# Prompt attention on one core: bias and minimum in one VectorE operation, fp32r scores, units ordered by pairs of heads

## The chip, the cores and the metric

The kernel runs on one core of a Trainium2 chip. The metric is the device time of one execution in microseconds; the profile is one further execution, recorded by the hardware profiler. PE is TensorE, DVE VectorE, ACT ScalarE, POOL GpSimd, SP the engine that issues most transfers.

## What is computed

The program is one step of a one-layer decoder with 1024 prompt tokens and 8 short samples. The change lies in the prompt's sparse attention (8 query heads, 2 groups of key heads, width 64) and in the projection that feeds it. For each head and token there are three softmaxes: over compressed blocks of keys (cmp), over all earlier keys (sel: the 16 blocks of 64 are all chosen at this length), and over a window of 512 (win):

```python
def masked_softmax(s, mask):
    s = jnp.where(mask, s.astype(jnp.float32), -1e30)
    m = jnp.max(s, axis=-1, keepdims=True)
    e = jnp.where(mask, jnp.exp(s - m), 0.0)
    return e / jnp.maximum(jnp.sum(e, axis=-1, keepdims=True), 1e-30)

def attend_shared(q, q_pos, k, v, k_pos, mask, rel_bias):
    s = jnp.einsum('...qgrd,...kgd->...qgrk', q, k).astype(jnp.float32) * (HEAD_DIM ** -0.5)
    dist = q_pos[..., :, None] - k_pos[..., None, :]
    bias = rel_bias[rel_bucket(dist)]
...
    p = masked_softmax(s + bias, mask[..., :, None, None, :])
    o = jnp.einsum('...qgrk,...kgd->...qgrd', p.astype(v.dtype), v)
    return o, p
```

The three outputs are weighted by gates and added.

## The kernel before

`program` runs seven stages in turn: projection, prompt attention, the state-space mixer (SSD), sample attention, output projection, and two feed-forward stages. Each stage is a block in which every engine has its own list of instructions, joined by semaphores that are written by hand; a block ends when all its engines have.

*Projection* (`stage_project`, L181). 17 column blocks of `w_in`, each in three pieces of 352 tokens, are multiplied on PE as fp32r parts (L470). Blocks of kind NORM give keys and queries; for each of their pieces ACT takes the square root (L680) and DVE a reciprocal (L937) and a scaling (L944, L955). Finished keys lie in `ev` by feature; SP copies them four times per branch, to both halves of the partitions of `m.kd` (`double_keys`, L370). At the end SP loads the bias table `m.bias` (L433) and the first queries (L177).

*Prompt attention* (`stage_prompt_attention`, L1437). A unit is one tile t of 128 tokens, one key group g and one pair of heads rp; there are 32, with tiles in the order 1, 3, 5, 7, 6, 4, 2, 0 and the four units of a tile one after the other. A unit has four steps i: sel for either head, then win with cmp for either head. Step n = 4u + i uses PSUM banks 0 and 1 or 2 and 3 by turns.

- `scores` (PE, L1566, L1569): the keys of a row are cut in half; either half is a matmul with 64 rows of the array, rows 0 to 63 or 64 to 127, in plain fp32. It waits until ACT's exponentials of step n - 2 have left the banks.
- `add_bias` and `prepare` (DVE): the bias is added in PSUM to the last 256 keys at most (L1704; farther keys all fall in the last bucket, which is subtracted from the table), the far mask to the first 128 of a full window, and the negated maximum is taken (L1714, L1717, L1719).
- `exps` (ACT, L1645, L1649): exponential from PSUM to the ring `psel` or `pwc` of three units, with the sum accumulated.
- `rate` (DVE, L1727, L1728) inverts the sums, and POOL multiplies the rows by that and the gate (L1671, L1676).
- Two units behind, `turn` (PE, L1582) transposes the rows in fills of two key tiles for both heads, `copy` (ACT, L1627) takes a fill from banks 4 to 6 to `pt` (4 slots), and `weigh` (PE, L1596) multiplies it with the values, adding into bank 7, from which `take_o` (DVE, L1734) takes a finished unit to `m.mix`. A unit of tile t has (t + 1) + min(t, 4) + 1 key tiles and one compressed one; tile 7 has 7 fills, all units together 160.

The order on PE is written out in one loop, with `LAG = 2` fills between a transpose and its weighting:

```python
for f in share(u - BEHIND, i):
    turn(u - BEHIND, f)
    behind.append((u - BEHIND, f))
    if len(behind) > LAG:
        weigh(*behind.popleft())
```

SP meanwhile loads queries for later tiles, gates by row (16 transfers), the samples' compression weights and states.

## Time and profile before

| | us |
|---|---|
| median of 3 runs | 1928.62 (1927.55 to 1933.23) |
| the profiled execution | 1937.85 |
| its span, first to last instruction | 1936.1 |
| PE busy in the span | 1781.6 (92%) |
| DVE busy | 1051.9 (54%) |
| ACT busy | 732.5 (38%) |
| POOL busy | 361.7 (19%) |

Times are microseconds, ns where marked. Busy PE counts a matmul from its start to a modelled end, and successive ones overlap, so start times tell more than durations. PE's matmuls are listed as PE, its weight loads as PEld. In lists by line, the columns are line, engine, operation, what is written and read, shapes, count, busy us, mean ns of one, and the idle time of the engine just before with what ended it.

### The profile page before, as it was taken

The numbers are of one execution on the slowest core, as the hardware profiler recorded it, in microseconds if no ns is written. First come the engines' busy times: TensorE is split into PE (matmuls) and PEld (weight loads), VectorE is DVE, ScalarE is ACT, GpSimd is POOL, SyncE is SP. The second block draws the span as 40 slices with busy tenths as digits, with TensorE's granted clock in tenths as the row PEclk, the third lists the DMA queues.
The fourth block names the chain that finished last, engine by engine and source line by source line (L and its number), as shares of the span: only waits on it lengthen the run. The fifth ranks groups of instructions, "written<-read, shape, count | busy, mean of one in ns | idle before, by whom it ended". The sixth has DMA issues, their size and how long they took to land. (4 is left out here: it accounts for less than half of the span.)

```text
span 1936.1 us, 33115 instructions
## 1 busy us (share of the span) xinstructions
PE 1781.6 (92%) x12217; PEld 1459.9 (75%) x12217; DVE 1051.9 (54%) x2339; ACT 732.5 (38%) x1546; POOL 361.7 (19%) x424
## 2 busy tenths in 40 slices
PE   6999997999999958998986997899999999899998
PEld 5999996666666645654654785899999999788885
DVE  6632167766666664556453457767677766541221
ACT  5413533676774233355332333333322332331111
POOL 1422111444344435325241000000000000100000
PEclk9999997899997988999988998899999999999999
DMA  5533141300000018637484322121222211832320
GB/s 149 98 119 86 36 99 29 66 12 12 13 14 1 6 43 321 199 131 267 154 276 155 122 80 90 53 79 66 87 77 69 96 66 45 324 92 60 98 90 24
DMA packets 160411, 188.92 MB, mean 98 GB/s; under 512 B 49727, under 2 KB 126184, under 8 KB 160235
## 3 DMA queue, kind: packets, MB, share of 16 engines
q1 hardware_dynamic: 139842, 114.00, 20.3%
q0 software_dynamic: 19872, 72.36, 10.8%
q8 instruction: 71, 1.16, 0.2%
q10 hardware_dynamic: 584, 1.06, 0.1%
q14 instruction: 42, 0.34, 0.1%
HBM read 156.30 MB, written 28.99 MB: 96 GB/s over the span
## 5 line engine op out<-in xcount | busy, mean ns | idle before, releaser
L2788 PE MATMUL banks<-u_sum,w_sum 128*128 128x264 f32 x3696 | 456.7, 286 | 16.3 <-DVE u_sum L2831 10.3
L2788 PEld LDWEIGHTS banks<-u_sum,w_sum 128*128 128x128 f32 x3696 | 455.5, 191 | 17.3 <-issue 9.1
L470 PE MATMUL banks<-u_parts_mix,w_in_parts 128*128 128x352 f32 x1440 | 244.3, 327 | 4.4 <-DVE u_parts_mix L826 4.4
L470 PEld LDWEIGHTS banks<-u_parts_mix,w_in_parts 128*128 128x128 f32 x1440 | 231.3, 189 | 7.8 <-DVE u_parts_mix L826 4.8
L3052 PE MATMUL banks<-w_down_hi,g_parts 128*128 128x512 f32 x704 | 218.9, 392 | 8.0 <-DVE g_parts L3087 8.0
L3052 PEld LDWEIGHTS banks<-w_down_hi,g_parts 128*128 128x128 f32 x704 | 133.1, 189 | 36.3 <-DVE w_down_lo L3083 7.7
L2088 ACT ACTIVATE turned<-banks 128x512 f32<-128x512 f32 (+1 forms) x136 | 78.7, 588 | 174.1 <-PE banks L1953 111.9
L1965 PE MATMUL banks<-turned,cmp_w 128*128 128x512 f32 x256 | 133.0, 601 | 7.2 <-DVE turned L2090 4.6
L3052 PE MATMUL banks<-w_down_lo,g_parts 128*128 128x512 f32 x352 | 137.7, 391 | 0.0
L3087 DVE TENSOR_TENSOR g_parts<-g_rows,g_parts 128x256 fp32r<-128x256 f32 (+1 forms) x99 | 39.1, 402 | 177.2 <-ACT g_parts L3020 177.0
L1953 PEld LDWEIGHTS banks<-consts,rows_grouped 128*128 128x128 f32 x512 | 64.7, 144 | 89.7 <-issue 58.8
L2961 POOL DMA_DIRECT2D w_down_whole<-in_w_down x10 | 5.3, 560 | 623.7 <-POOLq L129 623.7
L1627 ACT ACTIVATE p_T<-banks 128x512 f32<-128x512 f32 (+7 forms) x168 | 90.4, 543 | 64.3 <-PE banks L1582 63.4
L3020 ACT ACTIVATE g_parts<-g_rows 128x256 fp32r<-128x256 f32 (+1 forms) x99 | 38.6, 398 | 200.2 <-PE banks L3052 170.8
L1566 PE MATMUL banks<-keys_twice,q_twice 64*128 64x320 f32 (+7 forms) x512 | 99.5, 470 | 14.6 <-ACT p_win_cmp L1649 6.6
L1704 DVE TENSOR_TENSOR banks<-banks,bias 128x256 f32<-128x256 f32 (+6 forms) x240 | 64.2, 298 | 89.4 <-PE banks L1569 49.4
L2515 PE MATMUL banks<-w_out,mixT 128*128 128x512 f32 (+1 forms) x432 | 104.3, 399 | 5.8 <-DVE w_out L2536 5.8
L1953 PE MATMUL banks<-consts,rows_grouped 128*128 128x128 f32 x512 | 78.8, 279 | 30.5 <-DVE rows_grouped L2183 26.9
L2515 PEld LDWEIGHTS banks<-w_out,mixT 128*128 128x128 f32 (+1 forms) x432 | 77.4, 182 | 29.4 <-DVE w_out L2536 5.6
L1596 PE MATMUL banks<-p_T,v 128*64 128x128 f32 x1056 | 91.4, 294 | 2.6 <-DVE mix L1734 1.9
L1714 DVE TENSOR_REDUCE neg_max<-banks 128x1 f32<-128x640 f32 (+7 forms) x128 | 90.6, 708 | 4.4
L2725 ACT ACTIVATE w_sum<-w_whole 128x512 fp32r<-128x512 f32 x110 | 66.3, 623 | 69.5 <-DVE w_whole L2807 69.5
(404 smaller groups left out, 2817.9 us busy)
## 6 DMA issues: line engine op xcount, KB each, us to landing
w_gate_raw<-in_w_gate SPq DMA_DIRECT2D x11, 1024.0 KB, 5.6
w_up_raw<-in_w_up SPq DMA_DIRECT2D x11, 1024.0 KB
g_rows<-g_by_feature SPq DMA_DIRECT2D x88, 128.0 KB, 2.9
g_by_feature<-silu_gate SPq DMA_DIRECT2D x21, 528.0 KB, 3.2
w_in_raw<-in_w_in SPq DMA_DIRECT2D x29, 256.0 KB, 3.4
w_down_whole<-in_w_down SPq DMA_DIRECT2D x12, 512.0 KB, 11.5
w_down_whole<-in_w_down POOLq DMA_DIRECT2D x10, 512.0 KB, 16.4
x_tile<-in_x_prompt SPq DMA_DIRECT2D x8, 512.0 KB, 4.4
```

Source lines behind the costliest of these rows:

```text
L470: mm = nc.tensor.matmul(bank[:, 0:PIECE], w[:, pb, :], u[:, pa, k, tokens(p)], start=(k == 0 and (pa, pb) == TERMS[0]), stop=(k == KT - 1 ...
L1566: mm = nc.tensor.matmul(m.bank[2 * (n % 2) + h][:, 0:b - a], q[rows, :], m.kd[rows, branch, g, lo + a:lo + b], start=True, stop=True)
L1596: mm = nc.tensor.matmul(m.bank[7][64 * r:64 * r + 64, 0:P], x, pt[0:width, F % SLOTS_P, k, r, :], start=(br == SEL and kt == 0), stop=(br ...
L1627: x = nc.scalar.activation(to, have, ACT.Copy) if by_act[F] else nc.vector.tensor_copy(to, have)
L1714: x = nc.vector.tensor_reduce(negmax[:, u, r, br:br + 1], region(i, n, keys), AX.XY, ALU.max, negate=True)
L1953: x = nc.tensor.transpose(m.bank[3 + f % 3][0:width, k * P:(k + 1) * P], src, c("ident"))
L1965: mm = nc.tensor.matmul(m.bank[u % 2][:, :], m.cmp.w1[:, u % 2, q, :, :].rearrange("p j h -> p (j h)"), w.fill[:, f % SLOTS, :], start=(q ...
L2088: x = nc.scalar.activation(to, src, ACT.Copy)
L2515: mm = nc.tensor.matmul(m.bank[2 * (j % 2) + h][0:r, :], mT[:, j % 2, a, k, 0:r], wo[:, b, k, h * 512:(h + 1) * 512], start=(k == 0 and (a ...
L2725: nc.scalar.activation(wp[side, p][:, HI, :, :], src, ACT.Copy).then_inc(s.w_hi, 1)
L2788: mm = nc.tensor.matmul(bank(tg, i), wp[side, p][:, a, k, :], m.u[tg, i, b][:, k, :], start=(k == 0 and (a, b) == TERMS[0]), stop=(k == kh ...
L3052: mm = nc.tensor.matmul(m.bank[i.banks[h]][0:i.rows, :], gp[:, q % RG, pa, k, 0:i.rows], (whi, wlo)[pb][:, f, cols], start=(f == 0 and (pa ...
```

## The change

- **Scores** are fp32r. Queries are split by POOL into a high part and the rest (`split_queries`), keys into high parts on partitions 0 to 63 and low parts on 64 to 127 of `m.kd`, by ACT (`keys_hi`) and DVE (`keys_lo`) in the projection stage; the queries lie on both halves. A score is then two matmuls with all 128 rows, over up to 512 keys each. Keys are negated. SP's eight copies of keys are gone.
- **Bias and minimum.** The table holds the negated bias for the full width of 1024 keys (zero but for the last 256) of one pair of heads, in two slots. One fused DVE operation adds it to the negated scores, writes the sum to `psel` or `pwc` and keeps the minimum, which a second instruction writes out. ACT exponentiates there in place with scale -1. PE waits for `prepared` of step n - 2 instead of `exp_done`.
- **Units** go through all eight tiles for one pair of heads, then the next pair. The table of pair k is loaded by SP during pair k - 1 (8 transfers).
- **Weighted sums** are issued in bursts, when 6 fills have been transposed, of all but 2; `pt` has 8 slots, four of them in `m.mix`. Bank 7 has four places for outputs. Every fourth copy is DVE's.
- The samples' compression weights are loaded at the start of the SSD stage; `ssdn` moves into `m.mix`.

```diff
-Q_SLOTS = 4
+Q_RAW, Q_UNITS = 2, 4
 BCOPIES = 16
 T_ORDER = (1, 3, 5, 7, 6, 4, 2, 0)
-Q_PAIRS = [(t, g) for t in T_ORDER for g in range(NG)]
+HEAD_PAIRS = [(g, rp) for rp in range(2) for g in range(NG)]
+UNITS = [(t, g, rp) for g, rp in HEAD_PAIRS for t in T_ORDER]
...
+def load_table(sp, m, k, sem):
+    g, rp = HEAD_PAIRS[k]
+    for p0 in range(0, P, BCOPIES):
+        at = (g * REP + 2 * rp) * BCOPIES * BIASW + 127 - p0
+        sp.dma_start(m.table[p0:p0 + BCOPIES, k % 2, :, SEQ - 256:SEQ],
+                     bass.AP(m.negbias_dram.tensor, at, [[BIASW - 1, BCOPIES], [BCOPIES * BIASW, 2], [1, 256]])).then_inc(sem, 16)
...
+                def keys_hi(b):
+                    br, src = blocks[b][1] // 2 - 1, ev[:, slot_of[b], 3:3 + SEQ]
+                    act.wait_ge(s.keys_done, br + 1)
+                    if br == 0:
+                        act.wait_ge(s.cmp_summed, 2)
+                    nc.scalar.activation(m.kd[0:64, br, 0, :], src[0:64, :], ACT.Copy, scale=-1.0)
+                    nc.scalar.activation(m.kd[64:P, br, 1, :], src[64:P, :], ACT.Copy, scale=-1.0).then_inc(s.keys_hi, 1)
+                    nc.scalar.activation(m.kd[0:64, br, 1, :], src[64:P, :], ACT.Copy, scale=-1.0).then_inc(s.keys_split, 1)
...
+                def keys_lo(b):
+                    br, src = blocks[b][1] // 2 - 1, ev[:, slot_of[b], 3:3 + SEQ]
+                    dve.wait_ge(s.keys_hi, br + 1)
+                    nc.vector.scalar_tensor_tensor(m.kd[64:P, br, 0, :], src[0:64, :], -1.0, m.kd[0:64, br, 0, :].bitcast(F32),
+                                                   ALU.mult, ALU.subtract)
+                    nc.vector.scalar_tensor_tensor(m.kd[64:P, br, 1, :], src[64:P, :], -1.0, m.kd[64:P, br, 1, :].bitcast(F32),
+                                                   ALU.mult, ALU.subtract).then_inc(s.keys_split, 1)
...
-                sp.wait_ge(m.keys_in, 16 * 8)
-                sp.wait_ge(s.bias_stored, 16)
-                for p0 in range(0, P, BCOPIES):
-                    sp.dma_start(m.bias[p0:p0 + BCOPIES, :, :],
-                                 bass.AP(m.bias_dram.tensor, 127 - p0, [[BIASW - 1, BCOPIES], [BCOPIES * BIASW, NH], [1, 256]])
-                                 ).then_inc(s.bias_loaded, 16)
+                sp.wait_ge(s.bias_stored, 32)
+                sp.wait_ge(s.keys_split, 2 * 2)
                 sp.wait_ge(s.taken_v, taken_before[last_item[SECOND_Q]])
-                for q in range(2):
-                    double_queries(sp, m, q, 0).then_inc(m.q_first, 16)
-                    double_queries(sp, m, q, 0, 1).then_inc(m.q_first, 16)
+                for u0 in range(Q_RAW):
+                    for half in range(2):
+                        double_queries(sp, m, u0, half).then_inc(m.q_first, 16)
+                parted(sp, 2 * len(blocks) - 1)
+                for k in range(2):
+                    load_table(sp, m, k, s.bias_loaded)
...
-    LAG = 2
-    by_act = [True for F in range(first_fill[-1])]
+    LAG, TOGETHER_P, O_SLOTS = 2, 4, 4
+    by_act = [F % 4 != 3 for F in range(first_fill[-1])]
...
+    weighed_at, turned_at, pending = {}, {}, deque()
+    for u in range(U + BEHIND):
+        for i in range(4):
+            for f in share(u - BEHIND, i) if u >= BEHIND else ():
+                pending.append((u - BEHIND, f))
+            weighed_at[u, i] = []
+            if len(pending) >= LAG + TOGETHER_P or (u, i) == (U + BEHIND - 1, 3):
+                while len(pending) > (LAG if (u, i) != (U + BEHIND - 1, 3) else 0):
+                    weighed_at[u, i].append(pending.popleft())
...
                     t, g, rp = units[u]
-                    n, branch, r = 4 * u + i, i // 2, 2 * rp + i % 2
-                    q = qd[:, (u // 2) % QS, r, :]
...
+                    n, branch = 4 * u + i, i // 2
+                    pe.wait_ge(s.q_split, u + 1)
                     if n >= 2:
-                        pe.wait_ge(s.exp_done, n - 1)
-                    keys = (t + 1) * P if branch == 0 else win_tiles(t) * P
+                        pe.wait_ge(s.prepared, n - 1)
+                    keys = keys_of(t, branch)
                     lo = (t + 1) * P - keys
-                    for h, (a, b) in enumerate(halves(keys)):
-                        rows = slice(64 * h, 64 * h + 64)
-                        mm = nc.tensor.matmul(m.bank[2 * (n % 2) + h][:, 0:b - a], q[rows, :],
-                                              m.kd[rows, branch, g, lo + a:lo + b], start=True, stop=True)
+                    parts = [(m.bank[2 * (n % 2) + h][:, 0:b - a], m.kd[:, branch, g, lo + a:lo + b])
+                             for h, (a, b) in enumerate(halves(keys))]
                     if branch == 1:
-                        mm = nc.tensor.matmul(m.bank[2 * (n % 2)][:, 384:384 + cmp_keys(t)], q[0:64, :],
-                                              m.kcd[0:64, g, 0:cmp_keys(t)], start=True, stop=True)
+                        at = cmp_at(n)
+                        parts.append((m.psum[:, at:at + cmp_keys(t) + 1], m.kcd[:, g, 0:cmp_keys(t) + 1]))
+                    for out, k in parts:
+                        for part in (HI, LO):
+                            mm = nc.tensor.matmul(out, qs[:, u % Q_UNITS, part, i % 2, :], k, start=part == HI, stop=part == LO)
                     mm.then_inc(s.scored, 1)
...
-                behind = deque()
+                ended = 0
                 for u in range(U + BEHIND):
                     for i in range(4):
                         if u < U:
...
                         if u >= BEHIND:
                             for f in share(u - BEHIND, i):
                                 turn(u - BEHIND, f)
-                                behind.append((u - BEHIND, f))
-                                if len(behind) > LAG:
-                                    weigh(*behind.popleft())
-                while behind:
-                    weigh(*behind.popleft())
+                        if weighed_at[u, i] and ended:
+                            pe.wait_ge(s.o_taken, ended)
+                        for v, f in weighed_at[u, i]:
+                            weigh(v, f)
+                        ended += len(ends_at[u, i])
...
-                    if u >= RING_P:
-                        act.wait_ge(s.turned, first_fill[u - RING_P + 1])
-                    keys = (t + 1) * P if branch == 0 else win_tiles(t) * P
-                    br, dst = (SEL, psel) if branch == 0 else (WINB, pwc)
-                    x = nc.scalar.activation(dst[:, u % RING_P, r, 0:keys].rearrange("p (h k) -> p h k", h=2), region(i, n, keys),
-                                             ACT.Exp, bias=negmax[:, u, r, br:br + 1], accum_out=sums[:, u, r, br:br + 1])
+                    br, ring = (SEL, psel) if branch == 0 else (WINB, pwc)
+                    p = ring[:, u % RING_P, r, 0:keys_of(t, branch)]
+                    x = nc.scalar.activation(p, p, ACT.Exp, scale=-1.0, bias=negmax[:, u, r, br:br + 1],
+                                             accum_out=sums[:, u, r, br:br + 1])
...
+                def split_queries(u):
+                    if u >= Q_RAW:
+                        pool.wait_ge(s.q_loaded[u % Q_RAW], 32 * (u // Q_RAW))
+                    else:
+                        pool.wait_ge(m.q_first, 16 * 4)
+                    if u >= Q_UNITS:
+                        pool.wait_ge(s.scored, 4 * (u - Q_UNITS + 1))
+                    raw, part = qd[:, u % Q_RAW, :, :], qs[:, u % Q_UNITS, :, :, :]
+                    chain(nc.gpsimd.tensor_copy(part[:, HI, :, :], raw))
+                    nc.gpsimd.tensor_tensor(part[:, LO, :, :], raw, part[:, HI, :, :].bitcast(F32),
+                                            ALU.subtract).then_inc(s.q_split, 1)
+                split_queries(0)
+                nc.gpsimd.memset(m.table[:, :, :, 0:SEQ - 256], 0.0).then_inc(s.zeroed, 1)
+                for u in range(1, 3):
+                    split_queries(u)
...
-                def add_bias(u, i):
...
                 def prepare(u, i):
                     t, g, rp = units[u]
                     n, branch, r = 4 * u + i, i // 2, i % 2
+                    k = HEAD_PAIRS.index((g, rp))
+                    table = m.table[:, k % 2, r, :]
+                    keys = keys_of(t, branch)
+                    br, ring = (SEL, psel) if branch == 0 else (WINB, pwc)
+                    start, at = 1024 * (n % 2), cmp_at(n)
+                    if i == 0:
+                        if u >= RING_P:
+                            dve.wait_ge(s.turned, first_fill[u - RING_P + 1])
+                        if u == 1:
+                            dve.wait_ge(s.zeroed, 1)
+                        if k >= 2 and u % 8 == 0:
+                            dve.wait_ge(s.table_in[k - 2], 16 * (P // BCOPIES))
                     dve.wait_ge(s.scored, n + 1)
-                    add_bias(u, i)
-                    keys = (t + 1) * P if branch == 0 else win_tiles(t) * P
-                    br = SEL if branch == 0 else WINB
-                    x = nc.vector.tensor_reduce(negmax[:, u, r, br:br + 1], region(i, n, keys), AX.XY, ALU.max, negate=True)
                     if branch == 1:
-                        at = 1024 * (n % 2) + 384
-                        chain(nc.vector.tensor_reduce(negmax[:, u, r, CMP:CMP + 1], m.psum[:, at:at + cmp_keys(t)], AX.X,
-                                                      ALU.max, negate=True))
-                        x = nc.vector.tensor_scalar(negmax[:, u, r, CMP:CMP + 1], negmax[:, u, r, CMP:CMP + 1], 1e29, None,
-                                                    ALU.min)
-                    x.then_inc(s.prepared, 1)
+                        if t >= 4:
+                            old = m.psum[:, start:start + P]
+                            nc.vector.tensor_tensor(old, old, c("far"), ALU.subtract)
+                        chain(nc.vector.tensor_tensor_reduce(
+                            pwc[:, u % RING_P, r, CC:CC + cmp_keys(t)], m.psum[:, at:at + cmp_keys(t)],
+                            table[:, 927 - P * t:SEQ:16], 1.0, 3e38, ALU.add, ALU.min,
+                            negmax[:, u, r, CMP:CMP + 1]))
+                        nc.vector.tensor_scalar(negmax[:, u, r, CMP:CMP + 1], negmax[:, u, r, CMP:CMP + 1], 1e29, None,
+                                                ALU.min)
+                    mx = nc.vector.tensor_tensor_reduce(ring[:, u % RING_P, r, 0:keys], m.psum[:, start:start + keys],
+                                                        table[:, SEQ - keys:SEQ], 1.0, 3e38, ALU.add, ALU.min,
+                                                        negmax[:, u, r, br:br + 1])
+                    mx.then_inc(s.prepared, 1)
```

The order of PE in a unit of tile 7. Before (`keys_twice,q_twice` are scores, `consts,p_sel` transposes of the sel rows, `p_T,v` weighted sums):

```order
L1566 MATMUL banks<-keys_twice,q_twice 128x512 x2
L1582 MATMUL banks<-consts,p_sel 128x128 x4
L1596 MATMUL banks<-p_T,v 64x128 x4
L1566 MATMUL banks<-keys_twice,q_twice 128x512 x2
L1582 MATMUL banks<-consts,p_sel 128x128 x4
L1596 MATMUL banks<-p_T,v 64x128 x2
L1596 MATMUL banks<-p_T,vc 64x128 x2
L1582 MATMUL banks<-consts,p_sel 128x128 x4
L1596 MATMUL banks<-p_T,v 64x128 x4
L1566 MATMUL banks<-keys_twice,q_twice 128x320 x2
```

And with the change, in the second half of tile 7's unit and the start of tile 6's, whose fills are those of tiles 3 and 5 (`kc_parts` are the compressed keys):

```order
L1616 MATMUL banks<-consts,p_sel 128x128 x4
L1604 MATMUL banks<-key_parts,q_parts 128x512 x2
L1604 MATMUL banks<-key_parts,q_parts 128x128 x2
L1604 MATMUL banks<-kc_parts,q_parts 128x64 x2
L1616 MATMUL banks<-consts,p_win_cmp 128x128 x4
L1629 MATMUL banks<-p_T,v 64x128 x8
L1629 MATMUL banks<-p_T,vc 64x128 x2
L1629 MATMUL banks<-p_T,v 64x128 x4
L1604 MATMUL banks<-key_parts,q_parts 128x512 x2
L1604 MATMUL banks<-key_parts,q_parts 128x128 x2
L1604 MATMUL banks<-kc_parts,q_parts 128x64 x2
```

The weighted sums of several fills now follow one another, and scores and transposes of 128x128 operands stand together.

DVE in the same kind of unit. Before, one sel step and one win step:

```order
L1704 TENSOR_TENSOR banks<-banks,bias 128x256
L1714 TENSOR_REDUCE neg_max<-banks 128x1
L1734 COPY mix<-banks 128x128
L1704 TENSOR_TENSOR banks<-banks,bias 128x256
L1704 TENSOR_TENSOR banks<-banks,consts 128x128
L1704 TENSOR_TENSOR banks<-banks,bias 128x16
L1714 TENSOR_REDUCE neg_max<-banks 128x1
L1717 TENSOR_REDUCE neg_max<-banks 128x1
L1719 TENSOR_SCALAR neg_max<-neg_max 128x1
```

With the change (`ISA` rows are the fused operation and, with one element, its read-out):

```order
L1758 ISA p_sel,neg_max<-banks,bias_table 128x1024
L1758 ISA neg_max 128x1
L1775 COPY mix<-banks 128x128
L1751 TENSOR_TENSOR banks<-banks,consts 128x128
L1752 ISA p_win_cmp,neg_max<-banks,bias_table 128x63
L1752 ISA neg_max 128x1
L1756 TENSOR_SCALAR neg_max<-neg_max 128x1
L1758 ISA p_win_cmp,neg_max<-banks,bias_table 128x640
L1758 ISA neg_max 128x1
```

Three or four passes over PSUM have become one or two and a read-out each.

## Rows read from the trace of the kernel before

**Rows 1.** Head of the page: the profiled execution's span.

```profile
span 1936.1 us, 33115 instructions
```

**Rows 2.** Stretches of prompt attention: us, busy PE, PEld, DVE, ACT, POOL (count); clock; DMA.

```profile
316.80:327.00 10.20, 6.27 (x38) 5.23 (x39) 7.27 (x32) 5.17 (x17) 2.92 (x6) 0.50 0.32 77
...
327.00:347.00 20.00, 18.47 (x103) 12.91 (x100) 12.40 (x58) 9.89 (x38) 6.91 (x14) 0.50 0.06 14
...
416.00:464.00 48.00, 47.31 (x396) 29.73 (x396) 30.41 (x84) 33.24 (x80) 19.59 (x24) 1.00 0.06 13
...
586.00:603.00 17.00, 15.53 (x158) 11.37 (x159) 11.48 (x69) 11.40 (x46) 7.51 (x19) 1.00 0.01 2
...
603.00:618.30 15.30, 14.30 (x86) 9.36 (x86) 5.22 (x31) 5.84 (x23) 4.44 (x11) 0.50 0.00 1
```

**Rows 3.** Waits in 316 to 619: us in total, times, longest.

```profile
ACT p_T L1627 <- PE banks L1582: 63.4, 118, 2.0
...
PE banks L1566 <- ACT p_win_cmp L1649: 6.6, 8, 1.5
```

**Rows 4.** PE in order of time, a unit of tile 7: start, us, instructions.

```profile
438.70 1.13 PE L1566 MATMUL banks<-keys_twice,q_twice 64*128 64x512 f32 x4
...
451.24 1.13 PE L1566 MATMUL banks<-keys_twice,q_twice 64*128 64x512 f32 x4
...
452.30 0.66 PE L1582 MATMUL banks<-consts,p_sel 128*128 128x128 f32 x4
...
452.88 0.66 PE L1596 MATMUL banks<-p_T,v 128*64 128x128 f32 x8
...
453.47 1.13 PE L1566 MATMUL banks<-keys_twice,q_twice 64*128 64x512 f32 x4
...
457.27 0.81 PE L1566 MATMUL banks<-keys_twice,q_twice 64*128 64x320 f32 x4
...
458.17 0.66 PE L1582 MATMUL banks<-consts,p_sel 128*128 128x128 f32 x4
```

**Rows 5.** The same at tile 2.

```profile
554.48 0.60 PE L1566 MATMUL banks<-keys_twice,q_twice 64*128 64x192 f32 x4
555.00 0.66 PE L1582 MATMUL banks<-consts,p_sel 128*128 128x128 f32 x4
```

**Rows 6.** The same in the sample attention.

```profile
852.35 0.60 PE L1953 MATMUL banks<-consts,rows_grouped 128*128 128x128 f32 x4
852.79 1.02 PE L1965 MATMUL banks<-turned,cmp_w 128*128 128x512 f32 x2
```

**Rows 7.** L3052's matmuls (512 columns) in 1750 to 1800; the page's group L2788.

```profile
1750.00:1800.00 50.00, 50.00 (x222) 41.40 (x221) 1.00 0.30 88
...
L2788 PE MATMUL banks<-u_sum,w_sum 128*128 128x264 f32 x3696 | 456.7, 286 | 16.3 <-DVE u_sum L2831 10.3
```

**Rows 8.** VectorE's groups by shape: count, busy us, mean ns, idle before.

```profile
L1704 DVE TENSOR_TENSOR banks<-banks,bias 128x256 f32<-128x256 f32 x80 | 34.5, 431 | 66.0 <-PE banks L1569 36.4 <-PE banks L1566 29.3
...
L1714 DVE TENSOR_REDUCE neg_max<-banks 128x1 f32<-128x1024 f32 x8 | 9.8, 1225 | 0.3
...
L2090 DVE COPY turned<-banks 128x512 f32<-128x512 f32 x86 | 59.1, 691 | 61.3 <-PE banks L1953 58.1 <-PE banks L2011 1.5 <-issue 0.3
```

**Rows 9.** ScalarE's groups by shape.

```profile
L1627 ACT ACTIVATE p_T<-banks 128x512 f32<-128x512 f32 x128 | 76.4, 597 | 54.8 <-PE banks L1582 53.9
...
L1645 ACT ACTIVATION_READ_ACCUMULATOR p_sel<-banks,neg_max 128x1 f32 x64 | 12.6, 198 | 0.0
...
L1645 ACT ACTIVATE p_sel<-banks,neg_max 128x1024 f32<-128x1024 f32 x8 | 8.9, 1112 | 2.2 <-DVE neg_max L1714 2.2
```

**Rows 10.** GpSimd's subtraction of 512 columns.

```profile
L779 POOL TENSOR_TENSOR w_in_parts<-w_in_raw,w_in_parts 128x512 fp32r<-128x512 f32 x6 | 7.6, 1288 | 36.5 <-ACT w_in_parts L621 36.5
```

**Rows 11.** VectorE in the projection: a piece in order of time; the conv's row.

```profile
287.94 2.35 DVE L937 RECIPROCAL head_rstd<-head_rstd 128x352 f32<-128x352 f32 x1 [1.49 <-ACT head_rstd L680]
...
L840 DVE SCALAR_TENSOR_TENSOR conv_out<-columns,convw,conv_out 128x1024 f32<-128x1024 f32 x18 | 27.6, 1535 | 16.2 <-ACT conv_out L644 14.9
```

204 lines of the change are left out of this document (90 added, 114 removed).

## The prediction

> **What bounds the kernel now.** I read the page's head first (the profiled execution spans 1936.1 us [rows 1]), then the busy times stage by stage. Prompt attention runs from 316.8 to 618.3 us, 301.5 us in all, which I cut into stretches [rows 2]. In the stretch with the longest key rows (416 to 464) PE is busy 47.3 of 48 us, ACT 33, DVE 30, POOL 20. The list of waits agrees: ACT waits 63 us in all for transposes, PE 6.6 us for ACT, its longest sum [rows 3]. So PE's own stream of instructions is the clock of this stage, except at both ends: in 316.8 to 327 PE is busy 6.3 of 10.2 us, and there and up to 347 its granted clock is 0.50 (the 1.2 GHz level), as it is again from 603 [rows 2].
>
> Read PE in order of time in a unit of tile 7. A score group for 1024 keys takes 1.06 us up to the next group (451.24 to 452.30), one for 640 keys with its compressed keys 0.90 (457.27 to 458.17), a group of four transposes 0.58 (452.30 to 452.88) and its eight weighted-sum passes 0.59 [rows 4]. With 7 fills the unit needs 2 x 1.06 + 2 x 0.90 + 7 x 1.17 = 12.1 us, and its period is 451.24 - 438.70 = 12.5: the unit is PE work with 3% of waits.
>
> Why does a group of four transposes take 0.58? In the sample attention the same four transposes, followed by matmuls of the same 128x128 operand shape, take 0.44 (852.35 to 852.79) [rows 6], 0.11 each. In prompt attention they are followed by 128x64 ones, and these by 64x128 ones. Each change of shape thus costs about 0.15 us, and the present order changes shape at every group: 18 times in a unit of tile 7. The first instruction of each group also carries a semaphore wait, which is the other reading (a rival below).
>
> **The change part by part.**
> *Order of weighted sums, and shape of scores.* The sums now come in 37 bursts (counted in the new order), with 160 fills; transposes and scores both have 128x128 operands. Before, 320 transpose and sum groups held 0.15 us each, 48 us. Left are 37 x 2 changes, 11 us, and about 0.25 us per unit around the narrow transposes of the compressed keys, 8 us. Saved: 29 us. A fill costs PE 2 x 0.436 = 0.87.
>
> *fp32r scores.* Two half-height matmuls that ran side by side become two full-height passes per 512 keys. In the last stage 222 matmuls of 512 columns take 50 us, 0.225 each, and the 3696 of 264 columns 456.7 us, 0.124 each [rows 7]; for the short ones I take the transposes' 0.11 as floor, as each has weights of its own to load. 1024 keys: 4 x 0.227 = 0.91 instead of 1.06. 640 keys: 2 x 0.227 + 4 x 0.11 = 0.89 instead of 0.90. 384 keys (tile 2): 2 x 0.17 = 0.34 instead of 0.52 [rows 5]. Over eight tiles 3.3 us, times four: 13 us. No row shows an fp32r matmul under 264 columns: bounds are 0.11 and the four-pass price of plain fp32, 0.22 for 128 columns, up to 15 us dearer in all. I take 0.11, as the nearest rows scale with columns.
> The Trainium skill (TensorE: Matmul & The Clock Gate, section Back-to-back issue gap) gives about 131 ns per matmul of 512 columns in a sustained stream. The trace's row says 225 here; by that page's figure the 176 such score matmuls would be 17 us cheaper.
>
> PE in all: 160 x 1.17 + 128 score groups of 0.73 (an estimate between the 0.98 of tile 7 and the 0.52 of tile 2's selected scores) = 281 us before; 281 - 29 - 13 = 239 after.
>
> *VectorE.* The bias add (0.43 for 256 columns) goes; the reduction (1.225 for 1024) becomes a fused add-and-minimum that also writes to SBUF, plus a second instruction that reads the accumulator [rows 8]. Neither is in the trace. I take the fused one on the line through the two-input add at 256 and the reduction at 1024, 1.03 ns a column: two inputs in the one and a reduction in the other, at one rate. For the read-out I take 0.10, between 0 and ScalarE's 0.20 [rows 9]. A quarter of the copies moves here at 0.69 each, the row of another copy from PSUM [rows 8]. Tile 7 with the 5 fills of tile 3: 2 x 1.33, 2 x 1.66 (by the line 640 keys 0.83, the far mask 0.30, 63 compressed keys 0.23, and two read-outs and a short one), 1.0 of small ones and 1.25 copies of 0.69 make 7.9 us.
>
> *ScalarE* gives 40 of 160 copies away (0.60 each, 24 us); its exponentials (1.11 for 1024) are taken as equal from SBUF plus 0.03 [rows 9]: 7.4 us in that unit. *GpSimd* gets two instructions per unit to split queries, 1.3 us by a 128x512 subtraction of 1.29 [rows 10]: 6.3 us. Both run three units ahead and are covered by PE. If GpSimd's cover went (tiles 1 and 3, where all engines stand near 5 us), it would cost what the split costs, under 1 us a unit.
>
> *Order of units.* Tiles 1, 3, 5, 7, 6, 4, 2, 0 now follow each other four times, and the fills come two units behind, so I take the largest load of each pairing. In a steady pass: 5.4, 5.4 (DVE), 7.0 (DVE), 8.5, 9.3, 9.9, 8.6, 7.2 = 61.4 us, PE's where nothing is said. Four passes less 1.4 for the first one's missing fills, plus 6.2 of drain: 251 us. The same tally of the old order gives 289 against the measured 301.5; all of the difference lies at the two ends.
> On top of 251: 10 us (4%, for the closer race of the engines; tile 7 has 3% today), 2 us because scores wait for the first split, 4 us of PE at the lower clock in the third unit, 3 us of latency at the end. Stage: 270 us instead of 301.5.
>
> *Projection stage.* Eight key DMAs go; SP gets one more bias store and 16 small table loads for 8, some 8 us of issues that start behind its first query loads, before the last block of queries, and end before VectorE's last piece. VectorE gets four passes over 64x1024 keys at up to 1.54 us, ScalarE six of about 1.1, and VectorE waits for these. VectorE has 1.4 us to spare in each piece (its idle time before the reciprocal) [rows 11], so it falls about 5 us behind once and catches up; bounds 0 and 5 us of PE waiting. I take 1.5. In the attention stage SP's 16 gate DMAs stand ahead of the queries of unit 11, some 11 us against 25 of slack. Compression weights now load under the SSD stage, whose PE does not read them: nothing.
>
> Sum: 31.5 - 1.5 = 30 us less. The profiled execution took 1937.85 us and would take 1908; the median of the runs shown, 1928.62, lies 0.5% below that one, so I forecast 1899. My own range for this case is 1884 to 1916 (scores 15 dearer, races 0 to 10%, read-out 0 to 0.2 us).
>
> **The rivals.**
> *The fused operation is slow (slower than before).* If it takes two cycles an element, VectorE's 201 us become 272 and it is the largest load in nearly every unit; the tally rises from 251 to 292, and with 10 and 9 us the stage takes 311: 1940. It decides from about 1.75 cycles an element. Against it: the two-input add has one element a cycle with PSUM as a source [rows 8]. For it: it is the only operation here that nothing in the trace prices.
> The Trainium skill (Vector Engine (DVE) Microarchitecture Reference, section Points that are easy to get wrong) says that a related form with an accumulator halves its throughput when both sources are in SBUF and not bf16. Here one is in PSUM, and no row shows the case.
>
> *The race costs more, or the clock falls.* PE is no longer alone at the top: units of tiles 1, 3, 5 have PE at 80 to 90%. Before, the clock fell at 603 after a stretch with PE busy 15.5 of 17, and in 327 to 347 PE was busy 18.5 of 20 and stayed at the lower level [rows 2]. One such 15 us spell per pass costs 7.5 each, 22 to 30 us: about 1920. Against it: the new stream has fewer pauses inside a busy stretch.
>
> *The 0.15 us belongs to the waits.* Then bursts and equal shapes save little, since every group keeps its wait: PE 268 us. Some 20 of the 29 us come back in the end (PE then leads by more, and the 4% fall away): about 1920. Against it: [rows 6], where new lines follow at 0.44.
>
> *Long fp32r matmuls cost no more than the 264-column row's 0.124:* 176 x 0.10 = 18 us less, 1881. Against it: the row of 512 columns itself [rows 7].
>
> **How the numbers follow.** Forecast 0.66, slow fused operation 0.09, race or clock 0.13, waits 0.08, cheap scores 0.04. The measurement can tell 0.3%, 6 us. Faster: 0.66 + 0.04 + 0.15 of the two cases near 1920 = 0.85; within: 0.06; slower: 0.09. The range reaches from below the cheap scores to above the two cases near 1920: 1880 to 1926.
>
> **What would show it.** Right: unit periods near 10 us at tile 4; runs of transposes and sums spaced 0.11 with about 37 pairs of 0.2 gaps; score matmuls 0.227 at 512 columns; fused operation near 1.2 to 1.3 us at 1024; VectorE waiting for PE more than PE for VectorE. Wrong: PE waiting for VectorE's minimum in most units (slow fused operation), a granted clock of 0.50 in the middle of the stage, or 0.15 us still before each group.

## The result, and the profile after

| | before | after |
|---|---|---|
| median, us (4 runs each, same chip) | 1929.71 | **1877.01** (1872.41 to 1880.36) |
| ratio | | **0.9724**, 95% interval 0.9696 to 0.9751 |
| profiled execution, time / span, us | 1937.85 / 1936.1 | 1880.36 / 1878.1 |
| projection, first to last matmul | 303.9 | 303.1 |
| **prompt attention** | **301.8** | **245.3** |
| SSD / gap to the sample attention | 86.1 / 26.9 | 84.4 / 24.7 |
| sample attention / three stages behind it | 317.2 / 861.1 | 317.7 / 862.1 |

The forecast was 1899, with a range from 1880 to 1926: the right sign, but the gain is 53 us instead of 30, outside the range. The stage was to take 270 us and takes 245. The profiled spans differ by 58.0 us, of which 56.5 are in the stage and the rest is spread over rows that move by about 2 us at most; of the 27 us by which the profiled time lies under the forecast's 1908, 25 are in the stage.

Stretches of the changed kernel, with the columns of [rows 2]; the last two rows are the stage, cut where the clock rises:

```profile
span 1878.1 us, 32905 instructions
```

```profile
316.90:327.00 10.10, 9.26 (x29) 7.24 (x30) 6.56 (x34) 5.98 (x22) 8.11 (x12) 0.50 0.21 52
327.00:347.00 20.00, 19.50 (x158) 16.36 (x158) 15.18 (x50) 16.54 (x41) 17.96 (x28) 0.94 0.09 21
...
316.95:329.30 12.35, 11.56 (x37) 9.36 (x38) 8.63 (x39) 7.79 (x27) 10.28 (x16) 0.50 0.18 43
329.30:562.30 233.00, 227.90 (x2252) 193.02 (x2251) 148.61 (x640) 168.03 (x486) 147.79 (x240) 1.00 0.11 25
```

PE is busy 239.5 of 245.3 us, idle for 5.9, and at the lower level of its clock (0.50) for 12.4 us only. Before, it was busy 290.5 and idle 11.4, and 42.5 us of its work lay at 0.50 (24.7 up to 347 and 14.3 from 603 [rows 2], and 3.5 at 354, in the first of these two lines of before; the second is its long stretch at 1.00):

```profile
353.80:357.30 3.50, 3.50 (x20) 2.14 (x21) 1.30 (x3) 1.93 (x5) 2.25 (x4) 0.51 0.32 75
357.30:603.00 245.70, 242.07 (x2132) 159.95 (x2129) 163.49 (x546) 174.07 (x456) 103.08 (x152) 1.00 0.10 22
```

Within a group, transposes of 128 columns start 0.109 us apart at 1.00 and 0.21 at 0.50, so I estimate that half of such time is the clock's. That splits the 56.5 us into three: **PE's work at full clock 269.2 to 233.7 (35.5), the clock 21.3 to 5.8 (15.5), idle time 11.4 to 5.9 (5.5)**.

PE in order of time, a unit of tile 7 (the counterpart of [rows 4]):

```profile
511.81 1.20 PE L1604 MATMUL banks<-key_parts,q_parts 128*128 128x512 f32 x4
512.84 0.60 PE L1616 MATMUL banks<-consts,p_sel 128*128 128x128 f32 x4
513.20 1.18 PE L1604 MATMUL banks<-key_parts,q_parts 128*128 128x512 f32 x4
514.22 0.60 PE L1616 MATMUL banks<-consts,p_sel 128*128 128x128 f32 x4
514.57 0.88 PE L1604 MATMUL banks<-key_parts,q_parts 128*128 128x512 f32 x4
515.29 0.36 PE L1604 MATMUL banks<-kc_parts,q_parts 128*128 128x64 f32 x2
515.48 0.66 PE L1616 MATMUL banks<-consts,p_win_cmp 128*128 128x128 f32 x4
...
532.08 1.09 PE L1629 MATMUL banks<-p_T,v 128*64 128x128 f32 x16
533.01 0.82 PE L1629 MATMUL banks<-mix,v 128*64 128x128 f32 x12
```

Scores of 1024 keys take 1.03 us (511.81 to 512.84), not the 0.91 of the forecast and hardly less than the old 1.06. The four transposes behind them take 0.36, not 0.58 and not the 0.436 I took. The two together, from one score group to the next, take 1.39 us (511.81 to 513.20), against 1.64 before and 1.35 in the forecast; the starts alone do not tell how the gain splits between them. Sixteen sums, two fills with a wait for its copy ahead of each, take 0.93 us (532.08 to 533.01): 0.47 a fill instead of 0.59, at the same number of waits.

VectorE's and ScalarE's groups (compare [rows 8, 9]), and who waited longest for whom on PE:

```profile
L1758 DVE CUSTOM_DVE_ANT_0 p_win_cmp<-banks,bias_table 128x640 f32<-128x640 f32 x32 | 26.1, 814 | 0.0
...
L1758 DVE DVE_READ_ACCUMULATOR2_ANT neg_max<- 128x1 f32 x128 | 10.5, 82 | 0.0
...
L1758 DVE CUSTOM_DVE_ANT_0 p_sel<-banks,bias_table 128x1024 f32<-128x1024 f32 x8 | 9.7, 1217 | 4.4 <-PE banks L1604 4.4
```

```profile
L1675 ACT ACTIVATE p_sel<-p_sel,neg_max 128x1024 f32<-128x1024 f32 x8 | 9.2, 1152 | 5.5 <-DVE neg_max L1758 5.5
```

```profile
PE banks L1604 <- POOL q_parts L1705: 8.0, 3, 7.0
...
PE banks L1604 <- DVE neg_max L1758: 4.4, 11, 0.8
```

The fused operation takes 1.217 us for 1024 columns (forecast 1.23) and its read-out 0.082 (0.10). PE waits for VectorE 4.4 us in the whole stage; 7.0 of the 8.0 lie ahead of it. But VectorE's load was misread, as its instructions in order of time show:

```profile
437.23 0.69 DVE L1660 COPY p_T<-banks 128x512 f32<-128x512 f32 x1
437.83 0.17 DVE L1752 CUSTOM_DVE_ANT_0 p_win_cmp<-banks,bias_table 128x15 f32<-128x15 f32 x1
437.93 0.09 DVE L1752 DVE_READ_ACCUMULATOR2_ANT neg_max<- 128x1 f32 x1
```

Each starts before the one ahead of it has ended (437.23 + 0.69 is 437.92, the next starts at 437.83). The durations of VectorE's groups in the stage add up to 194 us, near my 201; the engine is busy for 157. The Trainium skill (VectorE: DVE Perf Modes, section Two Vector instructions with no wait between them) models when an instruction is held until all earlier ones are finished; one that is not held can start earlier. These rows agree with the latter, with 0.07 and 0.09 us of overlap.

### The profile page after: what moved, and what is told of

Read it like the earlier page. It is cut to its first block and busy times, and to the rows that moved or that the text cites. A ratio compares the mean times of both kernels' runs of the same rounds, so it can differ in the third digit from the quotient of the medians.

```text
span 1878.1 us, 32905 instructions
## 1 busy us (share of the span) xinstructions
PE 1728.7 (92%) x12089; PEld 1468.5 (78%) x12089; DVE 1018.0 (54%) x2341; ACT 713.1 (38%) x1512; POOL 397.5 (21%) x489
## 3 DMA queue, kind: packets, MB, share of 16 engines
q10 hardware_dynamic: 584, 1.06, 0.2%
## 5 line engine op out<-in xcount | busy, mean ns | idle before, releaser
L1604 PE MATMUL banks<-key_parts,q_parts 128*128 128x512 f32 (+3 forms) x384 | 100.0, 372 | 12.7 <-POOL q_parts L1705 8.0
L2131 DVE COPY turned<-banks 128x512 f32<-128x512 f32 x86 | 59.1, 690 | 60.2 <-PE banks L1994 57.6
L1604 PEld LDWEIGHTS banks<-key_parts,q_parts 128*128 128x128 f32 x384 | 65.1, 198 | 30.5 <-issue 13.5
L788 POOL TENSOR_TENSOR w_in_parts<-w_in_raw,w_in_parts 128x512 fp32r<-128x512 f32 (+1 forms) x39 | 54.6, 1418 | 139.2 <-ACT w_in_parts L619 139.2
L1725 POOL TENSOR_SCALAR p_win_cmp<-p_win_cmp,row_scale,gates 128x640 f32<-128x640 f32 (+12 forms) x128 | 70.4, 565 | 58.2 <-DVE row_scale L1768 58.2
```

What stands on the lines that cost most here:

```text
L788: nc.gpsimd.tensor_tensor(low, raw_of(q)[:, :, 0:width], wp[:, b % W_RING, HI, 4 * half:4 * half + 4, 0:width].bitcast(F32), ALU.subtract) ...
L1604: mm = nc.tensor.matmul(out, qs[:, u % Q_UNITS, part, i % 2, :], k, start=part == HI, stop=part == LO)
L1725: x = nc.gpsimd.tensor_scalar(p, p, scale[:, u, r, br:br + 1], gate(r, br), ALU.mult, ALU.mult)
L2131: x = nc.vector.tensor_copy(to, src)
```

## The experiments

Names with a_ start from the changed kernel, those with b_ from the kernel before. Each ratio is against the kernel before on the same chip. "Stage" is prompt attention in the profiled run, first to last matmul; idle is stage less PE's busy time. One profile each: I read nothing into 2 us. The profiles come from several chips; the stage, with nothing changed in it, took 244.4 us in a_warm_early on another chip, against 245.3. The profiled execution of before lay 8 us over its median, so differences of stages against 301.8 can be some us too large (for the kernels a_ the ratios give 2 to 7 us less gain); differences among the kernels a_ do not rest on it.

| run | ratio (95%) | stage | PE busy | idle |
|---|---|---|---|---|
| after | 0.9724 (0.9696 to 0.9751) | 245.3 | 239.5 | 5.9 |
| a_fill_by_fill | 0.9868 (0.9833 to 0.9902) | 271.6 | 269.0 | 2.6 |
| b_bursts | 1.0028 (1.0007 to 1.0049) | 304.7 | 276.0 | 28.7 |
| a_late | 0.9902 (0.9884 to 0.9921) | 279.6 | 247.9 | 31.7 |
| a_late_fills | 0.9927 (0.9908 to 0.9947) | 282.6 | 271.6 | 11.0 |
| a_scores_f32 | 0.9810 (0.9776 to 0.9844) | 260.0 | 257.1 | 2.9 |
| a_fills_f32 | 0.9888 (0.9868 to 0.9908) | 275.4 | 273.0 | 2.4 |
| a_late_f32 | 0.9946 (0.9930 to 0.9963) | 285.3 | 260.8 | 24.5 |
| a_late_fills_f32 | 0.9954 (0.9938 to 0.9971) | 286.3 | 276.4 | 10.0 |
| b_order | 1.0019 (0.9999 to 1.0038) | 305.0 | 288.3 | 16.7 |
| a_order_pairs | 0.9759 (0.9743 to 0.9775) | 249.8 | 240.9 | 8.9 |
| a_dve_more | 0.9772 (0.9737 to 0.9807) | 251.9 | 241.3 | 10.6 |
| a_copies_act | 0.9708 (0.9690 to 0.9725) | 242.9 | 238.2 | 4.6 |
| a_scores_hi | 0.9601 (0.9585 to 0.9617) | 223.3 | 207.7 | 15.6 |
| a_warm | 0.9743 (0.9725 to 0.9760) | 249.9 | 243.3 | 6.6 |
| b_warm | 1.0035 (1.0018 to 1.0052) | 309.0 | 298.1 | 10.9 |
| a_warm_early | 0.9732 (0.9715 to 0.9750) | 244.4 | 238.4 | 6.0 |

### Bursts, taken out and put in alone

a_fill_by_fill:

```diff
-                        if weighed_at[u, i] and ended:
-                            pe.wait_ge(s.o_taken, ended)
-                        for v, f in weighed_at[u, i]:
-                            weigh(v, f)
...
+                                behind.append((u - BEHIND, f))
+                                if len(behind) > LAG:
+                                    weigh(*behind.popleft())
...
```

> The changed kernel with its 37 bursts of weighted sums taken apart: transposes and sums alternate fill by fill again, two fills behind, as before. If a change of operand shape costs PE 0.15 us whatever waits stand there, 123 fills get two changes back: 123 x 0.28 = 34 us, and the time goes from 1877 to about 1911, with a group of four transposes back near 0.58 us and one of eight sums near 0.59. If the 0.15 us belonged to the semaphore waits (each fill keeps its wait in both kernels), the time stays within 4 us of 1877.

Measured: 26.3 us more in the stage (34 were expected), 29.5 more of PE work. PE in a unit of tile 7, and the stage:

```profile
530.78 1.20 PE L1604 MATMUL banks<-key_parts,q_parts 128*128 128x512 f32 x4
531.81 0.60 PE L1616 MATMUL banks<-consts,p_sel 128*128 128x128 f32 x4
532.34 0.66 PE L1631 MATMUL banks<-p_T,v 128*64 128x128 f32 x8
532.93 1.20 PE L1604 MATMUL banks<-key_parts,q_parts 128*128 128x512 f32 x4
```

```profile
316.69:588.28 271.59, 269.01 (x2288) 200.96 (x2288) 163.50 (x679) 184.40 (x513) 158.85 (x255) 0.98 0.10 23
```

The transposes are back at 0.53 us and the sums at 0.59. The cost follows the change of operand shape and not the waits. Over 123 fills it is 0.24 us a fill, or 0.12 a change. The Trainium skill (TensorEngine Tiling (Array Packing), section Key Properties) says that changing the tiling mode drains TensorE; these rows agree with that, the page gives no price for it, and my forecast should have named it.

b_bursts, the same part alone on the kernel before (8 slots, four sum regions, the changed kernel's burst table and loop):

```diff
-    SLOTS_P = 4
+    SLOTS_P = 8
...
-    LAG = 2
+    LAG, TOGETHER_P, O_SLOTS = 2, 4, 4
...
```

> The kernel before with the bursts alone (8 slots for transposed tiles, four sum regions, sums in bursts of four fills or more); scores, bias, exponentials and unit order as before. Its scores still have 64-row operands, so transposes between two score groups keep both changes of shape: about 3.5 changes a step become 2.3. Shapes theory: 155 changes of 0.15 us less, 23 us, so about 1906, or about 1896 if the clock also comes up earlier. Waits theory: 1925 to 1930.

Neither came: 3 us slower in the stage, and slower by the medians too.

```profile
315.56:620.27 304.71, 276.02 (x2416) 200.03 (x2416) 192.76 (x685) 195.07 (x553) 122.91 (x192) 0.91 0.10 22
```

```profile
PE banks L1584 <- ACT p_win_cmp L1666: 21.7, 26, 1.5
...
PE banks L1584 <- ACT p_sel L1662: 6.7, 17, 1.2
```

PE's work does fall by 14.5 us (290.5 to 276.0), but its idle time rises by 17, and it waits 28.4 us for exponentials where it was 8.4 (6.6 of it in [rows 3]). A bank of scores is free, in this kernel, only when ScalarE has read it. So I formed a new theory: what lets bursts count is line L1594 of the changed kernel, where PE waits for `prepared` and no longer for `exp_done`, since the exponentials no longer read PSUM.

### The release of the score banks

a_late puts that wait back; a_late_fills does so and also alternates fill by fill:

```diff
                     if n >= 2:
-                        pe.wait_ge(s.prepared, n - 1)
+                        pe.wait_ge(s.exp_done, n - 1)
```

> The changed kernel in which PE waits for the exponentials again before it writes the next scores into the same banks (the fused operation has by then already taken the scores out, so the wait is not needed; it is what the kernel before had). New theory after the bursts alone brought the kernel before nothing (PE busy 290 -> 276 us, but its idle time 11 -> 29): the early release of the score banks is what lets the bursts count. Then PE's idle time in the stage goes from 6 to 20 to 30 us and the stage from 245 to 260 to 270 us, the time to 1892 to 1902. Rival, the tally of my forecast, in which a wait of the kind was worth 4% at most and PE waited for the exponentials 6.6 us in all: 1879 to 1884.

> The same wait together with sums and transposes fill by fill (its twin without the wait took 271.6 us in the stage with 2.6 us of PE idle). New theory: with PE busy 269 us the exponentials come in time again, so the wait costs much less here: 3 to 10 us, stage 275 to 282, about 1910. If the late release costs the same in both, 285 to 297 us in the stage, about 1922.

```profile
316.83:596.43 279.60, 247.87 (x2288) 204.23 (x2288) 158.46 (x678) 179.38 (x513) 158.08 (x255) 0.97 0.10 22
```

```profile
PE banks L1604 <- ACT p_win_cmp L1679: 18.9, 22, 1.4
...
PE banks L1604 <- ACT p_sel L1675: 11.2, 18, 1.1
```

The wait costs **34 us** with bursts, more than the 15 to 25 I expected, and 11 without, just over the 3 to 10 expected. Seen the other way, bursts bring 26.3 us with the early release and 3.0 with the late one, though PE's work falls by 24 to 30 in both. The likely reason, which I argue from the order of the program: a burst leaves PE for 2.1 us on average without scores (37 bursts, the longest 2.6 us), and the steps between bursts are then shorter than the way scores, VectorE, ScalarE, with two score regions only. The early release cuts ScalarE, whose exponentials stand behind its copies, out of that way.

### The scores

a_scores_f32 writes scores as 64-row pairs in plain fp32 again. The first half of the keys meets the rounded keys, the second half reads the keys' remainders; the query remainders are left out.

```diff
...
-                        for part in (HI, LO):
-                            mm = nc.tensor.matmul(out, qs[:, u % Q_UNITS, part, i % 2, :], k, start=part == HI, stop=part == LO)
...
+                        mm = nc.tensor.matmul(out, qs[rows, u % Q_UNITS, HI, i % 2, :].bitcast(F32), k.bitcast(F32),
+                                              start=True, stop=True)
```

> The changed kernel with its scores as half-height plain fp32 matmuls again (64x512 pairs on the rounded keys and queries; the rounding remainders are left out of the scores). My working had 13 us for this part, 1890. If equal shapes of scores and transposes carry much of the gain as well (two changes of 0.15 us at each of 128 steps come back, less those at bursts), it is 13 + 28, about 1915. If the changed kernel were bound by VectorE in its small units, PE's extra work would be partly covered and the time would stay below 1890.

```profile
526.14 1.13 PE L1604 MATMUL banks<-key_parts,q_parts 64*128 64x512 f32 x4
527.20 0.65 PE L1617 MATMUL banks<-consts,p_sel 128*128 128x128 f32 x4
527.79 1.13 PE L1604 MATMUL banks<-key_parts,q_parts 64*128 64x512 f32 x4
```

14.7 us, near my 13, but changes of shape are in it (see a_fills_f32). By the starts the scores take 1.06 us (1.03 as fp32r) and the transposes behind them 0.59 (0.36), together 1.65 against 1.39. Pairs of kernels with the other parts undone, the scores as just shown:

> The changed kernel with sums fill by fill and half-height plain fp32 scores (remainders left out or misread, as in its twin with bursts). With bursts these scores cost 14.7 us in the stage (245.3 to 260.0), by the trace nearly all of it in the transposes behind them (0.59 us for four instead of 0.36 to 0.43) and little in the scores (1.06 for 1024 keys instead of 1.03). Fill by fill the transposes have a change of shape behind them anyway (0.53 us), so the plain scores should cost less here: 6 to 11 us, stage 278 to 283 instead of 271.6. If fp32r saved time in the score matmuls themselves, it is 13 us or more again: 285 or more.

> The changed kernel with plain fp32 scores and the late release of the score banks, with bursts. It is the nearest kin, in the new code, of the kernel before with bursts (304.7 us in the stage, 28.7 of it PE idle). Theory of the late release: idle time near 30 us again on PE work of 257, stage 285 to 292. Without that theory: 260 to 266.

> The changed kernel with all three parts undone: fill by fill, plain fp32 scores, late release. What it still differs in from the kernel before is the unit order, the fused operation with exponentials from SBUF and the copies on VectorE. Theory: the three parts together are nearly the whole gain and these others only bring the clock up earlier: stage 288 to 298 against 301.8. If order and fusion by themselves carried much of it: 275 to 285.

The eight kernels, each of three parts done or undone, make a cube; stage in us:

| | fp32r | plain fp32 |
|---|---|---|
| early release, bursts | 245.3 (the change) | 260.0 |
| early release, fill by fill | 271.6 | 275.4 |
| late release, bursts | 279.6 | 285.3 |
| late release, fill by fill | 282.6 | 286.3 |

Counted from the last kernel, with all three undone (286.3), each part alone brings 1 (bursts), 4 (fp32r) or 11 us (release); together they bring 41. fp32r brings 3.8 fill by fill, less than the 6 I expected at least: there the sums behind the transposes change the shape anyway. a_late_f32 came within my bounds: there bursts take 15.6 us from PE's work and add 14.5 of idle time, as they took 14.5 and added 17 in b_bursts. So the late release is the likely reason why b_bursts failed; on the kernel before itself the early release was not tried, as its exponentials read PSUM. With all three undone the stage is still 15.5 us shorter than before (I expected 4 to 14), though the ratio of 0.9954 makes it 6 to 12 us of the whole time:

```profile
317.82:332.50 14.68, 11.03 (x49) 7.21 (x50) 7.53 (x38) 7.00 (x26) 11.23 (x17) 0.50 0.19 45
332.50:604.16 271.66, 265.33 (x2368) 176.93 (x2368) 155.73 (x642) 178.57 (x488) 146.74 (x238) 1.00 0.09 21
```

PE's work at full clock is 270.8 us (276.4 less half of 11.0) against 269.2, its idle time 10.0 against 11.4. What differs is the work at 0.50, 11.0 us against 42.5: half of that is 15.7, the whole rest.

### The order of the units

b_order gives the kernel before the new order alone (with queries loaded unit by unit):

```diff
+UNITS = [(t, g, rp) for g, rp in HEAD_PAIRS for t in T_ORDER]
...
-    units = [(t, g, rp) for t, g in pairs for rp in range(2)]
+    units = UNITS
...
```

> The kernel before with the new order of units alone (tiles 1, 3, 5, 7, 6, 4, 2, 0 for each pair of heads, four times; queries loaded unit by unit). With bursts, fp32r scores and early release all undone, the changed kernel still took 286.3 us in the stage against 301.8; PE's work at full clock is the same in both (271 and 269 us) and so is its idle time (10 and 11), but 42.8 us of PE's work in the kernel before lay at the lower clock and 11.1 in the other. If it is the order that keeps PE from four small units in a row at both ends, the low clock shrinks here in the same way: stage 286 to 291, about 12 us less. If it is the fused operation and the shorter way from scores to exponentials, it stays at 298 to 303.

```profile
317.42:334.60 17.18, 12.42 (x52) 7.82 (x52) 12.01 (x44) 8.39 (x26) 4.79 (x9) 0.50 0.13 31
402.90:409.70 6.80, 6.58 (x25) 3.37 (x26) 3.82 (x10) 3.80 (x11) 3.09 (x6) 0.50 0.05 12
478.00:491.60 13.60, 12.93 (x54) 7.05 (x53) 7.34 (x22) 6.61 (x19) 4.18 (x6) 0.50 0.04 10
```

The theory falls, and 305.0 us lies over both ranges. The clock does rise 12 us earlier (334.6 instead of 347), and it no longer falls at 603. But it now falls three times in the middle, where small units of two passes meet (the third time from 556.5 to 559.9), so that 35.3 us of PE's work still lie at 0.50, and idle time grows from 11.4 to 16.7: no gain. With the same order a_late_fills_f32 holds 1.00 from 332.5 to the end. So the earlier rise comes with the order, and what keeps the clock up in the middle is among the other differences, the fused operation with exponentials from SBUF and the shared copies. Which of them it is, and what they would bring in the old order, I did not separate.

a_order_pairs puts two pairs of heads side by side at each tile of the changed kernel:

```diff
-UNITS = [(t, g, rp) for g, rp in HEAD_PAIRS for t in T_ORDER]
+UNITS = [(t, g, rp) for half in range(2) for t in T_ORDER for g, rp in HEAD_PAIRS[2 * half:2 * half + 2]]
```

> The changed kernel with units of two pairs of heads side by side at each tile (order 1, 1, 3, 3, 5, 5, ... twice instead of 1, 3, 5, ... four times), so that units of like size meet more often; the bias tables of the second half load at the middle. Tally of largest loads: 247 instead of 251, 4 us less. If PE is the bound throughout, the order is worth nothing, and the table loads in the middle cost some 2 to 4 us: 1877 to 1881.

4.5 us more in the stage, with the clock at 0.50 from 443.8 to 450.6, near the middle where the tables are exchanged; PE waits there for weights by GpSimd, 2.8 us at once. The tally had 4 us less: it had the wrong sign. The edit moves the table loads too, and order and loads were not separated.

### VectorE, ScalarE and what comes next

a_dve_more:

```diff
+                    for j in range(2):
+                        nc.vector.tensor_reduce(spare[:, 2 * n + j:2 * n + j + 1], c("ident"), AX.X, ALU.max)
```

> The changed kernel with two more reductions of 128 columns (0.29 us each in the trace of before) on VectorE in each of the 128 steps, ahead of the fused operation, their results unused. My forecast took VectorE as the largest load of three units in eight by the sum of its durations; then 8 x 0.29 = 2.3 us a unit raise the tally by 35 us, and the time to about 1905 to 1912. If VectorE's instructions overlap (157 us of the stage busy in the trace against 194 us of summed durations) and PE is the bound everywhere, the dose is 0.2 us each and mostly covered: 5 to 15 us more, 1882 to 1892.

```profile
317.58:569.47 251.89, 241.29 (x2288) 202.45 (x2288) 204.56 (x932) 179.41 (x513) 158.84 (x255) 0.97 0.11 25
```

47 us more of VectorE's time cost 6.6, within the 5 to 15 expected of the overlap and far from the tally's 28 to 35. VectorE was not the bound of three units in eight (two, as the prediction marks them).

a_copies_act (`by_act = [True for F in ...]`):

> The changed kernel with all 160 copies of transposed tiles on ScalarE, as before (VectorE 27 us less, ScalarE 24 us more, 200 of 245 us in the stage). Tally of largest loads: 2.5 us less. PE as the only bound: no difference up to 5 us more, where ScalarE's copies come later for PE's next transposes.

The stage is 2.4 us shorter and the time at least as good; VectorE's share of the copies is not part of the gain. The tally had 2.5 us less, but a difference of that size decides nothing.

a_scores_hi leaves out the remainder of the queries in the scores:

```diff
-                        for part in (HI, LO):
-                            mm = nc.tensor.matmul(out, qs[:, u % Q_UNITS, part, i % 2, :], k, start=part == HI, stop=part == LO)
+                        mm = nc.tensor.matmul(out, qs[:, u % Q_UNITS, HI, i % 2, :], k, start=True, stop=True)
```

> The changed kernel without the second pass of each score matmul (the remainder of the queries is left out of the scores). It takes about 45 us of work from PE and nothing from the others. If PE is the only bound (239 us busy of 245 in the stage), most of it shows until ScalarE (176 us busy) and VectorE (157) come near: 30 to 40 us, 1837 to 1847. By the tally that takes VectorE's durations as its load the gain ends at 22 us, about 1855.

```profile
PE banks L1603 <- DVE neg_max L1757: 11.6, 21, 1.3
```

PE's work falls by 31.8 us, the stage by 22.0: idle time is back at 15.6 and the clock falls twice (434.8 to 445.0 is the longer stretch). 45 us for the pass was too much, and with PE relieved the others begin to show: PE waits 11.6 us for VectorE's minima, where it was 4.4. The 22 us are what the tally had and not the 30 to 40 of PE as the only bound, so PE's lead over the others is small. This does not make the tally right, whose load for VectorE a_dve_more refutes; it says that taking work from PE alone stops paying soon. It is the fastest kernel of the study, at the price of that remainder.

### The clock at the start

a_warm and b_warm add 60 transposes at the head of the stage, as shown; a_warm_early adds 50 behind PE's last instruction of the projection:

```diff
+                for _ in range(60):
+                    nc.tensor.transpose(m.bank[7][:, 0:P], c("ident"), c("ident"))
```

> The changed kernel with 60 more transposes on PE at the head of prompt attention, in the 7 us in which it waits for the first split queries. If the clock stays at 1.00 over the gap, the 11.6 us that PE is busy at 0.50 in 317 to 329 become about 6: 5 to 6 us less, about 1871. If the low clock there costs nothing because these units are bound by latency, 1877. If the clock falls all the same, 1877 too, with 0.50 in the row.

> The kernel before with the same 60 transposes in the same gap. In its trace PE is busy 24.7 us at 0.50 in 317 to 347 and 3.5 more at 354. If that is what its slow start costs, 10 to 14 us less: 1915 to 1919, so that 5 to 9 us of the change's gain is the earlier clock and not its smaller work. If the start is bound by latency: 1925 to 1929.

> The changed kernel with 50 more transposes behind PE's last instruction of the projection stage (310 us), in the 6 us before the next stage begins; the ones placed at the head of attention began only at 316 and delayed it by 8 us, of which the higher clock gave back 3.4. If the clock stays at 1.00 over the gap and the small first units hold it, the stage takes 240 to 242 us instead of 245: 4 us less. If not, no difference.

The first two missed their aim: PE enters the stage only at 316, so the transposes ran for 8 to 9 us and delayed it. The clock rose at 319.0 and stayed in a_warm (the units behind them took 3.4 us less); in b_warm it rose at 320.8 and was back at 0.50 from 327.6 to 354.9, a stretch in which the small units leave PE idle for 4.0 of 27.3 us. a_warm_early filled the gap but for its last 2.0 us (up to 317.56):

```profile
309.90:318.80 8.90, 6.53 (x56) 6.07 (x55) 5.88 (x9) 2.07 (x3) 2.41 (x3) 1.00 0.00 0
318.80:329.00 10.20, 9.17 (x29) 7.42 (x30) 6.56 (x35) 6.71 (x25) 8.13 (x15) 0.50 0.21 52
```

The clock fell at 318.8 all the same and rose at 329.0, as without them. a_warm's 3.4 us are what the higher clock gave the units at the start, of 5.8 by the estimate above; no run kept that gain.

## Why the prediction was wrong

**What bounds the kernel.** Right: PE before and after.

**Order of weighted sums, shape of scores (29 us).** About right in its own terms: a change of shape costs 0.12 us where I took 0.15, and the bursts take 29.5 us from PE's work. With plain scores they take only 15.9 (273.0 to 257.1), so this needs the scores' new shape too. What I left out is the condition. I wrote of the early release nowhere in the change part by part; I costed it at nothing, and without it bursts that take 24 us from PE's work are worth 3 in the stage.

**fp32r scores (13 us).** Too much. Fill by fill, where the transposes have a change of shape beside them in any case, fp32r takes 4.0 us from PE's work (273.0 to 269.0) and 3.8 from the stage. The 14.7 us of a_scores_f32 are near 13 by luck, for they hold changes of shape, which the forecast had under the 29. Both parts together take 4.0 + 29.5 = 33.5 us from PE and 30.1 from the stage (275.4 to 245.3), not 42.

**Scores in detail.** "1024 keys: 4 x 0.227 = 0.91" measured 1.03, and the four transposes 0.36 and not 0.436; together 1.39 for a forecast of 1.35. PE's sum of 239 after met 239.5 by luck: 5.8 of these are the lower clock, so the work at full clock is 233.7. The 281 of before was 12 too high (269.2), and the saving is 35.5 instead of 42.

**VectorE.** Single durations right (1.217 for 1.23, 0.082 for 0.10). The sum of 201 us failed as a load: 194 of durations are 157 of time. The overlap could be seen in the trace of before, where the stage has 223 us of durations and 196 busy. ScalarE's exponentials took 0.04 more (I took 0.03), GpSimd's split 1.13 us a unit for 1.3.

**Order of units: this is the step that failed.** The stage was forecast as a tally of largest loads, 251, plus 10 for the race, 2 for the first split, 4 for the clock and 3 at the end, 270. That is 239 of PE's own work, 12 by which the tally lies above it, 15 of waits and 4 of clock. The stage measured 233.7 of PE's work at full clock, 5.9 of idle time in place of these 12 and 15, and 5.8 of clock. The tally let VectorE bound two units in eight (three, as a_dve_more's expectation counts them), which a_dve_more refutes. The 10 us for the race scaled up "3% of waits" in tile 7's unit, the difference of 12.5 and 12.1 us; but in that unit PE's one idle time over 0.15 us is 0.17, and from 357.3 to 603 the kernel before is idle for 3.6 of 245.7 us. Of its 11.4 us of idle time 8.4 are waits for exponentials, most of them at the ends, and the change takes that wait away.

The old order's clock is the other side. Before, the clock rose at 347 and fell at 603; after, it rises at 329 and stays, 15.5 us. The forecast had put 12.5 us on the ends of the old order (289 to 301.5) and 9 on those of the new, 3.5 less. The earlier rise goes with the order (b_order); why the clock then stays up is open.

**Projection stage (1.5 us).** Nothing of it: 303.1 us against 303.9.

**The rivals.** The fused operation is not slow. The race is cheaper than forecast and the clock did not fall after 329. That the 0.15 us belong to waits is refuted by the sixteen sums in 0.93 us and by a_fill_by_fill. Cheap scores would have given 1881, near the result, but 1024 keys take 1.03 us and not half that: the right number for a wrong reason.

The profiled spans differ by 58 us, the medians by 52.7, for the profiled execution of before lay 8 us over its median and that of after 3. The granted clock of the whole execution goes with this: the profile of before has 0.956, and in the 13 executions of before beside a_fill_by_fill the three at 0.956 took 1930 to 1935 us, the two at 0.961 and 0.962 took 1926 and 1923. So part of the 15.5 us of clock may be this execution's own; in which stages it lies, one profile of before can't tell.
